# A macaron trunk layer in fp32: first groups that start from the tokens' upper left quarter

## The reference

```python
def rmsnorm(x, w):
    y = x * lax.rsqrt(jnp.mean(x * x, axis=-1, keepdims=True) + NORM_EPS)
    return y * w
def swiglu(h, w_gate, w_up, w_down):            # 1024 -> 2816 -> 1024
    return (silu(h @ w_gate) * (h @ w_up)) @ w_down
x = x + 0.5 * swiglu(rmsnorm(x, ffn1_norm), ffn1_w_gate, ffn1_w_up, ffn1_w_down)
x = x + sink_window_attention(rmsnorm(x, mix_norm), w_qkv, b_qkv, sinks, w_o, b_o)
x = x + 0.5 * swiglu(rmsnorm(x, ffn2_norm), ffn2_w_gate, ffn2_w_up, ffn2_w_down)
out = rmsnorm(x, final_norm)
```

## Time and profile before

| | us |
|---|---|
| median of 3 runs | 1596.69 (1596.25 to 1596.81) |
| profiled execution | 1597.06 |
| its span | 1595.2 |
| PE busy | 1574.4 |
| DVE busy | 1065.7 |
| ACT busy | 700.8 |

### The profile page before, as it was taken

How to read it: one execution, slowest core, us unless ns; L and a number is a source line. 1 busy time by engine, 2 the same in 40 slices (tenths; PEclk the granted TensorE clock), 3 DMA queues, 4 the chain that set the end, 5 groups by cost and what they waited for, 6 DMA issues and landing times.

```text
span 1595.2 us, 21792 instructions
## 1 busy us (share of the span) xinstructions
PE 1574.4 (99%) x7432; PEld 1311.5 (82%) x7432; DVE 1065.7 (67%) x1827; ACT 700.8 (44%) x1438; POOL 58.7 (4%) x51
## 2 busy tenths in 40 slices
PE   6999999999999999999999999999999999999998
PEld 5888888888888888888888888888888888888886
DVE  7965556555468755953789877766555555497666
ACT  7533333333244444633677755433333333344454
POOL 0000000000000000050222100000000000000000
PEclk9999999999999999999999999999999999999999
DMA  5333222222485333443212422333233331874343
GB/s 175 112 134 124 99 99 99 99 99 99 151 327 188 112 93 99 126 101 85 53 54 67 158 94 80 108 119 103 99 107 117 114 110 73 298 247 137 94 133 119
DMA packets 157734, 195.59 MB, mean 123 GB/s; under 512 B 43616, under 2 KB 96992, under 8 KB 157664
## 3 DMA queue, kind: packets, MB, share of 16 engines
q1 hardware_dynamic: 157664, 194.69, 37.5%
HBM read 145.89 MB, written 48.76 MB: 122 GB/s over the span
## 4 chain that ended last, share of the span: by engine, by line
PE 94%; DVE 3%; DMA 1%; issue 1%; ACT 0%; SPq 0%; DVEq 0%; ACTq 0%
PE bank L601 91%; PE bank L822 1%; PE bank L631 1%; PE bank L836 1%; DMA stage_u<-in_ffn_w_up 1%; DVE slot L1516 1%; DVE raw L1507 0%; PE bank L750 0%; DMA x_res<-in_x 0%; DVE forms L1428 0%; DVE x_res L1391 0%; DMA a_raw<-hidden_forms 0%; DVE buf L1524 0%; DVE hn L1445 0%; DVE x_res L1448 0%
## 5 line engine op out<-in xcount | busy, mean ns | idle before, releaser
L601 PE MATMUL bank<-forms,slot 128*128 128x512 f32 x3744 | 852.8, 390 | 0.5 <-DVE buf L1535 0.3
L601 PEld LDWEIGHTS bank<-forms,slot 128*128 128x128 f32 x3744 | 702.6, 188 | 147.0 <-issue 0.8
L601 PE MATMUL bank<-b_ring,a_ring 128*128 128x512 f32 x1848 | 420.7, 389 | 0.1
L601 PEld LDWEIGHTS bank<-b_ring,a_ring 128*128 128x128 f32 x1848 | 346.5, 188 | 72.3 <-DVE b_ring L1559 0.6
L1001 ACT ACTIVATE buf<-bank 128x512 f32<-128x512 f32 x120 | 71.5, 598 | 333.5 <-PE bank L601 332.3
L1524 DVE TENSOR_TENSOR buf<-buf,bank 128x512 f32<-128x512 f32 x120 | 82.1, 686 | 181.7 <-PE bank L601 94.3
L1019 ACT ACTIVATE a_ring<-a_raw 128x512 fp32r<-128x512 f32 x154 | 97.0, 630 | 210.9 <-DMA a_raw<-hidden_forms 210.8
L1556 DVE TENSOR_TENSOR a_ring<-a_raw,a_ring 128x512 fp32r<-128x512 f32 x154 | 106.0, 689 | 108.7 <-ACT a_ring L1019 108.3
L601 PE MATMUL bank<-w,hT 128*128 128x512 f32 (+1 forms) x576 | 117.0, 359 | 0.6 <-DVE w L1363 0.6
L601 PE MATMUL bank<-hT,w 128*128 128x512 f32 x480 | 114.3, 394 | 0.0
L601 PEld LDWEIGHTS bank<-w,hT 128*128 128x128 f32 x576 | 93.6, 189 | 15.9 <-DVE w L1363 0.8
(11 more groups left out here) (125 smaller groups left out, 1196.7 us busy)
## 6 DMA issues: line engine op xcount, KB each, us to landing
a_raw<-hidden_forms SPq DMA_DIRECT2D x154, 256.0 KB, 2.7
hidden_forms<-buf SPq DMA_DIRECT2D x148, 256.0 KB, 2.1
stage_g<-in_ffn_w_gate SPq DMA_DIRECT2D x22, 1024.0 KB, 5.4
stage_u<-in_ffn_w_up SPq DMA_DIRECT2D x22, 1024.0 KB, 7.9
down_w<-in_ffn_w_down SPq DMA_DIRECT2D x16, 1024.0 KB, 8.8
x_res<-in_x SPq DMA_DIRECT2D x16, 512.0 KB, 8.2
stage_qkv<-in_attn_w_qkv SPq DMA_DIRECT2D x32, 256.0 KB, 3.7
stage_o<-in_attn_w_o SPq DMA_DIRECT2D x64, 128.0 KB, 2.9
```

The source lines that it names most:

```text
L601: mm = pe.matmul(psum, lhs, rhs, start=(first and n == 0 and v == 0), stop=(last and n == len(parts) - 1 and v == 2), skip_group_check=True)
```

## The change

The gain vector of the first norm is loaded as one row of 4 KB by a DMA that ACT issues, spread over 128 rows by two matmuls of a column of ones with it, and copied by DVE to `norm_w` in halves. In feed-forward 0 the first four tiles are normed in halves, left ones first (`left_done`), with the scales of tiles 2 and 3 made as a pair; PE turns A11 alone before it begins, and A12 between the first steps. The pieces 0 to 3 are split straight from PSUM and copied to x_res afterwards. The first group's weights are loaded in four parts, rows 0 to 511 first (`early_loaded`), for both feed-forwards. The order of products puts both left-form products first (b = 0 and 2), with new bank numbers and waits to match. The norms of the last four tiles go in pairs, the last forms go ahead of the third block's hidden product, and at the end the left half of the last tile is stored by a DMA of ACT. Left out below: new semaphores, the indices of a few waits (`BLOCK_DONE`, `PLAIN_GATE_DONE`), and unchanged lines.

```diff
--- before.py
+++ after.py
...
-PLAIN = [(A11, 0), (A12, 1), (A11, 2), (A12, 3), (A21, 0), (A22, 1), (A21, 2), (A22, 3)]
+PLAIN = [(A11, 0), (A11, 2), (A12, 1), (A12, 3), (A21, 0), (A21, 2), (A22, 1), (A22, 3)]
+BLOCK_AT = [0, 2, 1, 3]
+BLOCK_DONE = [4, 6, 5, 7]
+PLAIN_GATE_DONE = [5, 7, 13, 15]
...
     probs_T_lo = at("probs_T_lo", 204, [P, 2, 4 * P], F32R)
+    norm_row = at("norm_row", 192, [1, D])
+    ones_row = at("ones_row", 196, [1, P])
...
                                  ).then_inc(gate_up_loaded, 16)
...
+            def load_first_stage(q):
...
+                for half in range(2):
+                    for m, weights in enumerate((gates[q], ups[q])):
+                        sp.dma_start(stage[m][:, 4 * half:4 * half + 4, :],
+                                     weights[half * HALF:(half + 1) * HALF, 0:GROUP].rearrange("(k p) c -> p k c", p=P)
+                                     ).then_inc(gate_up_loaded if half else early_loaded, 16)
...
             load_x(x, 4)
-            load_norm(ffn1_norm, 0)
...
                 load_x(x, t)
-            load_stage(0, 0)
+            load_first_stage(0)
...
             sp.wait_ge(scores_done, 32)
-            load_stage(1, 0)
+            load_first_stage(1)
...
             t = tile_of(N_FINAL + TT - 1)
-            for dh, finished in enumerate((last_scaled, last_finished)):
-                sp.wait_ge(finished, 1)
-                cols = slice(dh * HALF, (dh + 1) * HALF)
-                sp.dma_start(out[t * P:(t + 1) * P, cols], hn[:, (TT - 1) % 4, cols]).then_inc(stored[(TT - 1) % 4], 16)
+            sp.wait_ge(last_finished, 1)
+            sp.dma_start(out[t * P:(t + 1) * P, HALF:D], hn[:, 3, HALF:D]).then_inc(stored[3], 16)
...
         def _(pool):
+            pool.memset(ones_row[:, :], 1.0).then_inc(ones_ready, 1)
...
                     pe.wait_ge(ident_ready, 2)
-                pe.wait_ge(hn_done, m + 1)
+                if v < 4 and not q:
+                    pe.wait_ge(left_done, j + 1)
+                else:
+                    pe.wait_ge(hn_done, m + 1)
...
                 form, b = PLAIN[p]
-                pe.wait_ge(slot_ready, slots_before(q, 1) - 8 + 2 * b + m + 1)
-                pe.wait_ge(form_ready, FORMS * q + [4, 8, 8, 8, 16, 16, 16, 16][p])
-                if p == 0 and q:
-                    pe.wait_ge(exp_done, 32)
-                if p in (4, 6):
-                    pe.wait_ge(hidden_done, 4 * GROUPS * q + (1 if p == 4 else 2))
-                three_passes(banks[m if p in (0, 1, 4, 5) else 2 + m][:, :],
+                pe.wait_ge(slot_ready, slots_before(q, 1) - 8 + 2 * BLOCK_AT[b] + m + 1)
+                pe.wait_ge(form_ready, FORMS * q + [4, 4, 8, 8, 15, 15, 16, 16][p])
+                if p == 0:
+                    pe.wait_ge(exp_done, 32) if q else pe.wait_ge(norm_w_loaded, 16)
+                if p == 1 and q:
+                    pe.wait_ge(form_kept, 8 * q + 8)
+                if p in (4, 5):
+                    pe.wait_ge(hidden_done, 4 * GROUPS * q + p - 3)
+                three_passes(banks[2 * (p % 2) + m][:, :],
...
                                (forms[:, FORM_AT[form], 0, kt, :], forms[:, FORM_AT[form], 1, kt, :]))
-                              for kt in range(4)], p % 2 == 0, p % 2 == 1).then_inc(gate_up_done, 1)
+                              for kt in range(4)], p % 4 < 2, p % 4 >= 2).then_inc(gate_up_done, 1)
...
                 plain_step(q, 0, 0)
+                if not q:
+                    blocks(q, 4, 6)
                 plain_step(q, 0, 1)
+                if not q:
+                    blocks(q, 6, 8)
...
                 mm.then_inc(turned, 1)
-            for v in range(8):
+            pe.wait_ge(ones_ready, 1)
+            pe.wait_ge(norm_row_loaded, 16)
+            for dh in range(2):
+                pe.matmul(banks[dh][:, :], ones_row[:, :], norm_row[:, dh * HALF:(dh + 1) * HALF], start=True, stop=True
+                          ).then_inc(norm_row_spread, 1)
+            for v in range(4):
...
                 form, j = form_of(v)
-                if v < 8:
+                if v < 4 and not q:
+                    act.wait_ge(form_turned, v + 1)
+                    src = banks[turn_bank(q, v)][:, :]
+                elif v < 8:
...
                 if v == 28:
-                    act.wait_ge(gate_up_done, steps_before(q, 1) - 2)
+                    act.wait_ge(gate_up_done, steps_before(q, 1) - 4)
...
                 for m in range(2):
-                    act.wait_ge(gate_up_loaded, 32 * (GROUPS * q + 1))
+                    if b % 2:
+                        act.wait_ge(gate_up_loaded, 32 * (GROUPS * q + 1))
+                    else:
+                        act.wait_ge(early_loaded, 32 * (q + 1))
...
                         form_hi_of(q, v)
-                plain_hi(q, 0)
+                if q:
+                    plain_hi(q, 0)
+                plain_hi(q, 2)
                 if not q:
-                    keep_and_split(q, 3, 8)
+                    for v in range(4):
+                        keep(q, v)
+                square(0)
+                square(1)
+                root(m, 2)
+                if not q:
+                    keep_and_split(q, 4, 6)
                 plain_hi(q, 1)
-                square(0)
-                root(m)
-                square(1)
-                root(m + 1)
-                plain_hi(q, 2)
+                if not q:
+                    keep_and_split(q, 6, 8)
                 square(2)
-                root(m + 2)
+                square(3)
+                root(m + 2, 2)
...
                 plain_hi(q, 3)
-                square(3)
-                root(m + 3)
...
                 slot_hi_of(q, 0, 1, 0, True)
+                his(24, 32)
...
                 slot_hi_of(q, 0, 1, 1, True)
-                his(24, 32)
...
                 group(q, 0, GROUPS - 1, last=True)
+            act.dma_start(norm_row[:, :], ffn1_norm.rearrange("(o n) -> o n", o=1)).then_inc(norm_row_loaded, 16)
...
             act.activation(stat[:, ROOT, 0:1], stat[:, RSTD, 0:1], ACT.Sqrt)
-            for j in range(4):
...
+            def square_first(j):
...
                 square_to(j, junk[:, :])
-                root(j)
-                if j >= 2:
-                    keep_and_split(0, j - 2, j - 1)
-            keep_and_split(0, 2, 3)
...
+            square_first(0)
+            root(0)
+            square_first(1)
+            root(1)
+            form_hi_of(0, 0)
+            square_first(2)
+            square_first(3)
+            root(2, 2)
+            form_hi_of(0, 1)
+            plain_hi(0, 0)
+            form_hi_of(0, 2)
+            form_hi_of(0, 3)
...
             act.activation(hn[:, 3, 0:HALF], hn[:, 3, 0:HALF], ACT.Copy, scale=stat[:, RSTD, 3:4]).then_inc(last_scaled, 1)
+            t = tile_of(N_FINAL + TT - 1)
+            act.wait_ge(last_scaled, 1)
+            act.dma_start(out[t * P:(t + 1) * P, 0:HALF], hn[:, 3, 0:HALF]).then_inc(stored[3], 16)
...
                                          in1=norm_w[:, :], op0=ALU.mult, op1=ALU.mult).then_inc(hn_done, 1)
+            def normed_half(j, half):
...
+                cols = slice(half * HALF, (half + 1) * HALF)
+                dve.wait_ge(norm_w_loaded, 16)
+                dve.wait_ge(rstd_done, j + 1)
+                h = x_res[:, tile_of(j), cols]
+                dve.scalar_tensor_tensor(out=h, in0=h, scalar=stat[:, RSTD, j:j + 1], in1=norm_w[:, cols],
+                                         op0=ALU.mult, op1=ALU.mult).then_inc(hn_done if half else left_done, 1)
...
                 for m in range(2):
-                    dve.wait_ge(slot_hi, slots_before(q, 1) - 8 + 2 * b + m + 1)
+                    dve.wait_ge(slot_hi, slots_before(q, 1) - 8 + 2 * BLOCK_AT[b] + m + 1)
...
                         form_lo_of(q, v)
-                def scale(j):
-                    rstd(m + j)
-                    normed_form(q, 4 + j)
...
-                plain_lo(q, 0)
+                if q:
+                    plain_lo(q, 0)
+                    before(0)
+                    before(1)
+                    plain_lo(q, 2)
+                else:
+                    los(1, 2)
+                    plain_lo(q, 0)
+                    los(2, 4)
+                    normed_half(0, 1)
+                    normed_half(1, 1)
+                    plain_lo(q, 2)
+                    normed_half(2, 1)
+                    normed_half(3, 1)
+                before(2)
+                before(3)
+                rstd(m, 2)
+                normed_form(q, 4)
                 if not q:
-                    los(3, 8)
+                    los(4, 6)
+                normed_form(q, 5)
                 plain_lo(q, 1)
-                before(0)
-                before(1)
-                scale(0)
-                plain_lo(q, 2)
-                before(2)
-                scale(1)
-                before(3)
-                scale(2)
+                if not q:
+                    los(6, 8)
```

(38 more changed lines are left out.)

## The result

The changed kernel takes 1599.81 us, median of 14 runs (1598.73 to 1600.48); the kernel before took 1596.72 in 14 runs beside it (1596.24 to 1596.84). The ratio is 1.002, 95% interval 1.0013 to 1.0027: slower by 3.1 us, where 1596.8 was forecast, within 1594.8 to 1599.0. The profiled execution took 1599.56, its span 1597.6, so 2.5 and 2.4 above the profiled one of before. The runs of the changed kernel lie 1.75 us apart, those of before 0.6. One run of one experiment (the last stores, in the kernel before) took 1760.67 us at a granted clock of 0.85 and is left out of its ratio.

A forecast was written before the change was run, and what follows sets the result against it. TensorE, busy 99% of the span, was taken as the bound. Terms +0.4 (start), -0.15 (idle spell) and -0.1 (tail) sum to +0.15; 1597.06 + 0.15 - 0.37 (profiled run to median) = 1596.8 us, range 1594.8 to 1599.0.

The forecast's parts named there:

- Step 1: Start, gain row: lands at 3.3, two spreading matmuls take 1.8; first scaling at 7.35 us in place of 6.92.
- Steps 2 and 3: Start, half scaling, block turns, then ACT's and DVE's chain: first product at 18.1 us, was 20.73, gain 2.6.
- Step 4: First products: 16 turns of right halves' blocks 4 to 7 come between them, unhidden, costing 1.74 us.
- Step 5: First products: PE at its low level until the clock rises at 22.2 us, losing 2.05 us, before 0.76.
- rival B: First two steps: clock rises only at 24.1 us, +0.95 over the forecast, time 1597.8; chance 0.22.
- D: Start: the two spreading matmuls are slow; +0.5, 1597.3, or 1597.6 if FP32 takes four passes; chance 0.06.
- eighth step: End of PE's first eight steps: 47.3 us, before 46.89, so +0.4.
- The rest of the first groups: After the first products: PE's new waits on ACT and DVE all hidden, with 1.3 us or more.
- The -0.15: PE's idle spell at 96.01 us, ahead of late-loaded weights, goes away: -0.15 us.
- The tail: Last stores: ACT issues the left half's store; between 0 and -0.4 us, taken as -0.1.
- slower by over 3.2 us: Whole kernel: slower by over 0.2%, from blocked SP issues, half of the unseen and rival B's tail; chance 0.07.

## Why the prediction was wrong

**Step 1, the gain vector: the step that failed.** The landing was right (3.3 forecast, 3.2 found). The term "two are 1.8" measured 3.75, 1.95 over. Hand-overs, last copy and scale took 0.5 less than I had counted, so the first scaling came at 8.80, 1.45 over the forecast 7.35 and beyond its late end of 8.4. The price in time is 1.3 and 1.5 us by the two experiments that take the wait away.

I had taken the cold turns as the upper row and called them the nearer kind, and let the scores speak against more. The scores' row was misread. Its 16 records are not 16 matmuls: `scores` issues 8 for each block, and the kernel's 128-column scores are 120 matmuls where the trace has 240 records at L822. So each takes two records, as the spreading matmuls do here, and 136 ns, not 68; and consecutive ones use different halves of the rows, so a lone one may well take longer (not shown). Scaled to 512 columns at the low level it is 1.09 us for one and 2.2 for two, above my 1.8. The row spoke for the slow case, not against it.

The page "FP8 and Floating Point Precision" of the Trainium skill (Matmul Precision, TensorE Precision Notes) states four passes for true FP32: an estimate of 3.4 us for the two at 1.2 GHz. The trace agrees: the copies that wait for one matmul each begin 1.70 us apart, four times the 0.427 of a product at the low level, and the whole is 0.35 over the estimate.

**Steps 2 and 3** were right: from the first scaling to the first product 10.95 us, forecast 10.75. So the first product came at 19.75 for 18.1, 1.45 of it from step 1.

**Step 4**, the moved turns, was right: 0.87 for each pair of blocks.

**Step 5, the clock.** The loss was 1.74, and 0.27 more for the first product behind a pause, which I had put at nothing; forecast was 2.05. That the sizes agree is luck: the rise that I had fixed at 22.2 came near 23.5, towards rival B, and the later start shortened the slow stretch. It is no fixed moment. With the wait gone the profiled loss was 2.4 in the products and 0.3 in the turns in one version (18.11), 1.9 in the other (17.95). The kernel before differs too: 0.76 lost in the profiled run, and 0.06 in the run with only the last store changed, whose 48 products take 10.96 in the chain for 11.66. I should have treated B and D as two things that add and not as cases that exclude each other; 19.75 + 27.14 + 2.0 = 48.9 for the eighth step is near what happened (48.99), and the range stopped at 1599.0.

Eighth step: 48.99 for 47.3. Of the 1.7, 1.45 are from step 1 and 0.2 from steps 2 and 3.

**The rest of the first groups.** No turn waited for ACT or DVE, as forecast. The -0.15 came at 96 us and was taken back by the 0.32 at 111.87: +0.18 for -0.15, 0.33 off. The stall of 0.32 is in every version with the new order, and in the kernel before once it has idle turns. I read it as belonging to an undisturbed second group, as in the second feed-forward; no run tests that.

**The tail.** +0.14 for -0.1 in the profile; the medians of the two experiments show nothing.

**From one run to the median.** I took 0.37 off because the profiled run of before lay that much over its median. That of the changed kernel lay 0.25 under its own. I read the 0.62 as the clock's run-to-run share: 0.06 to 0.76 in two traces of the kernel before, 1.7 to 2.8 in three of the changed order without idle turns. That it is smaller before because most turns stand just ahead of the products is argued, not shown.

In all: 1.7 to the eighth step, 0.33, 0.24, 0.62, and 0.1 around the span make the 3.0 by which the forecast was short.

The direction, slightly slower, was in the text, but "slower by over 3.2 us" was given 0.07 and the measured 3.1 stands at its edge. What stays open is what places the clock's rise in a run. With the row off the path the changed kernel is still 1.6 to 1.8 over before. Idle turns take 2.6 from the version with the gain vector by SP, so there the low clock was more than the whole of it. What is left is 0.8 and 0.7 under before, in two versions on two chips; all 22 runs lie below every run of before beside them, though each interval still holds 1.

## What to carry to other kernels

A faster start for TensorE is worth only what its clock then gives: behind scattered turns and a pause of 1.74 us the first products ran at the low level, behind dense turns and pauses of 0.64 to 1.18 us at the high one. So look at what TensorE did ahead of them, and at the distance between runs, which shows that price varying. Before you take a price from a row, count its records against the instructions that the kernel issues: here 16 records were 8 matmuls. Before a small transfer is swapped for a matmul, find who waits for its result: the same gain row was nearly free in one order of norms (+0.13) and cost 1.3 to 1.5 us in another, and splitting the wait in halves gave that back with a few lines. And an idle gap is a cheap place for turns that nobody reads, as long as they can't hold up a real one at the low level.

## What the runs showed of the hardware

- Two plain fp32 matmuls of one row by 128 and 512 columns take 3.75 us at the low clock, their results 1.70 apart, and each shows as two records. Seven idle turns ahead of them, themselves at the low level (1.75 us for 7), left them at 3.78. The scores, plain fp32 on 64 rows and 128 columns, are two records each too, 8 in 1.09 us at the high level. A turn of an fp32 block is one record.
- The granted clock reads 1.00 from the start of the trace, also where turns are 226 ns apart and products 427; only the spacing shows the level of 1.2 GHz at the start.
- Turns alone bring the high level: in the version with the gain vector by SP and idle turns, 22 of them took 2.56 us ahead of any product.
- The level also falls back between turns: in the kernel before with idle turns PE stood idle for 2.08 us ahead of block 0, whose four turns took 0.63 us; the ten idle turns right behind took 2.25, the low level.
- The same row of 4 KB landed after 1.46 us in one run and 2.39 in another.
